# Transposing the turned keys once and copying them to both row halves out of PSUM

## The reference, cut to what matters

```python
def global_axial_attention(q, k, v, q_gain, k_gain, ang2d):
    ...
    q = apply_rope(rms_norm(q, q_gain, QK_EPS), ang2d) * (HEAD_DIM ** -0.5)
    k = apply_rope(rms_norm(k, k_gain, QK_EPS), ang2d)
    ...
        s = jnp.einsum('bqkgd,bskd->bkgqs', qblk, k)
        p = jax.nn.softmax(s, axis=-1)
        return jnp.einsum('bkgqs,bskd->bqkgd', p, v)

def window_sink_attention(q, k, v, sink, ang1d):
    ...
    k = apply_rope(k, ang1d)
    ...
        s = jnp.einsum('bqkgd,bskd->bkgqs', qblk, kblk)
        s = jnp.where(mask, s, -jnp.inf)
```

## Time and profile before

| | |
|---|---|
| three runs | 1204.88, 1205.07, 1205.17 us; median 1205.07 us |
| the profiled execution | 1204.98 us, span 1203.0 us, so 1.98 us around the span |
| busy share of the span | PE 99%, PEld 81%, POOL 49%, DVE 44%, ACT 40% |
| mean granted TensorE clock | 0.998 of full speed |

### The profile page before, as it was taken

How to read it: one execution, slowest core, us unless ns; L and a number is a source line. 1 busy time by engine, 2 the same in 40 slices (tenths; PEclk the granted TensorE clock), 3 DMA queues, 4 the chain that set the end, 5 groups by cost and what they waited for, 6 DMA issues and landing times.

```text
span 1203.0 us, 16482 instructions
## 1 busy us (share of the span) xinstructions
PE 1186.2 (99%) x5784; PEld 971.0 (81%) x5784; DVE 524.5 (44%) x1094; ACT 483.5 (40%) x890; POOL 585.3 (49%) x338
## 2 busy tenths in 40 slices
PE   7999999999999999999999999999999999999997
PEld 6787778888888888888888777788888888888886
DVE  7777857522121234211587788374221122431107
ACT  3457763244343333323144777433443343332310
POOL 6565754455444444343254756634554443434330
PEclk9999999999999999999999999999999999999999
DMA  6321213344333332223132202333433333322301
GB/s 223 87 71 54 89 53 106 122 125 138 97 95 87 105 106 88 88 92 104 54 80 79 73 34 71 140 105 88 140 106 103 99 93 96 97 74 102 105 35 70
DMA packets 121753, 113.45 MB, mean 94 GB/s; under 512 B 6752, under 2 KB 97888, under 8 KB 121696
## 3 DMA queue, kind: packets, MB, share of 16 engines
q1 hardware_dynamic: 121696, 112.71, 30.1%
HBM read 110.60 MB, written 2.10 MB: 94 GB/s over the span
## 4 chain that ended last, share of the span: by engine, by line
PE 95%; DVE 1%; POOL 1%; DVEq 1%; DMA 1%; issue 0%; SPq 0%
PE ps L1238 29%; PE ps L1240 28%; PE ps L1239 28%; PE ps L1404 3%; PE ps L1390 3%; PE ps L1378 1%; PE ps L1380 1%; PE ps L1248 1%; PE ps L1361 1%; POOL w_lo L544 1%; DMA x<-in_x_prompt_dram 1%; POOL ln_r L540 0%; DVEq L886 0%; DVEq L932 0%; PE ps L1415 0%
## 5 line engine op out<-in xcount | busy, mean ns | idle before, releaser
L534 POOL TENSOR_TENSOR w_lo<-raw,w_hi 128x1024 fp32r<-128x1024 f32 x188 | 453.1, 2412 | 404.6 <-ACT w_hi L645 404.5
L1238 PE MATMUL ps<-xt_hi,w_hi 128*128 128x512 f32 x704 | 273.9, 389 | 0.0
L1239 PE MATMUL ps<-xt_lo,w_hi 128*128 128x512 f32 x704 | 273.9, 389 | 0.0
L1240 PE MATMUL ps<-xt_hi,w_lo 128*128 128x512 f32 x704 | 273.9, 389 | 0.0
L645 ACT ACTIVATE w_hi<-raw 128x1024 fp32r<-128x1024 f32 x188 | 197.8, 1055 | 132.2 <-PE ps L1240 61.4
L1238 PE MATMUL ps<-w_hi,stat 128*128 128x512 f32 x480 | 187.8, 391 | 0.0
L1239 PE MATMUL ps<-w_lo,stat 128*128 128x512 f32 x480 | 187.1, 390 | 0.0
L1240 PE MATMUL ps<-w_hi,stat 128*128 128x512 f32 x480 | 187.1, 390 | 0.0
L1238 PEld LDWEIGHTS ps<-xt_hi,w_hi 128*128 128x128 f32 x704 | 132.2, 188 | 27.5
L1239 PEld LDWEIGHTS ps<-xt_lo,w_hi 128*128 128x128 f32 x704 | 132.2, 188 | 27.4
L1240 PEld LDWEIGHTS ps<-xt_hi,w_lo 128*128 128x128 f32 x704 | 132.2, 188 | 27.3
(11 more groups left out here) (123 smaller groups left out, 1323.7 us busy)
## 6 DMA issues: line engine op xcount, KB each, us to landing
raw<-in_w_up_dram SPq DMA_DIRECT2D x88, 512.0 KB, 3.8
raw<-in_w_down_dram SPq DMA_DIRECT2D x44, 512.0 KB, 3.2
raw<-in_w_in_dram SPq DMA_DIRECT2D x22, 512.0 KB, 3.7
raw<-in_w_out_dram SPq DMA_DIRECT2D x16, 512.0 KB, 3.3
raw<-in_w_ple_gate_dram SPq DMA_DIRECT2D x16, 512.0 KB, 3.3
scratch<-in_ln_g_dram SPq DMA_DIRECT2D x5, 512.0 KB, 4.1
scratch<-in_ln_b_dram SPq DMA_DIRECT2D x5, 512.0 KB, 6.0
raw<-in_w_ple_dram SPq DMA_DIRECT2D x4, 512.0 KB, 3.3
```

The costliest lines, as they stand in the source:

```text
L534: pool.tensor_tensor(w_lo[:, n, :], raw[:, n % RAW, :], w_hi[:, n, :].bitcast(F32), ALU.subtract).then_inc(w_split.sem, 1)
L1238: pe.matmul(out, a[0], b[0], start=first, stop=False)
L1239: pe.matmul(out, a[0], b[1], start=False, stop=False)
L1240: return pe.matmul(out, a[1], b[0], start=False, stop=last)
```

## The change

The kept keys are written once by `rotate`: 128 columns where 256 stood. In `rot` of stripes 1 and 2 TensorE then transposes three blocks, with the two key heads in one of them, head `v` in rows 64 v to 64 v + 63. `qkt_evac` copies each head to both row halves by itself: four copies of 64 rows by 128 columns (head v = 0, 1, to half odd = 0, 1), and `qkt_lo` makes the four low parts likewise. Nothing else is changed: the queries' copies, the semaphores and the order of the steps stay.

```diff
-        def k_parts(c, u):
+        def k_part(c, u, v):

             at = 0 if c == 1 else 256
-            first = 4 * (c - 1)
-            return (ps[:, TRB + u % 2, at:at + 256].rearrange("p (v n) -> p v n", v=KV), slice(first, first + 2),
-                    slice(first + 2, first + 4))
+            return ps[HD * v:HD * v + HD, TRB + u % 2, at:at + P]
+
+        def k_home(c, v, lo, odd, t):
+
+            return k_split[HD * odd:HD * odd + HD, k_block(c - 1, v, lo), t * P:(t + 1) * P]
...
                     if c:
-                        src, hi_at, _ = k_parts(c, u)
-                        act.activation(k_split[:, hi_at, cols_t], src, ACT.Copy)
+                        for v in range(KV):
+                            for odd in range(2):
+                                act.activation(k_home(c, v, 0, odd, t), k_part(c, u, v), ACT.Copy)
...
-                        dve.tensor_tensor(out[:, 0:256].rearrange("p (v e d) -> p v e d", v=KV, e=2),
...
+                        dve.tensor_tensor(out[:, 0:128].rearrange("p (v d) -> p v d", v=KV),
...
-                        dve.tensor_tensor(out[:, 0:256], bank[:, 0:256], turned[:, 0:256], ALU.add)
...
-                        dve.tensor_tensor(out[:, 256:512].rearrange("p (v e d) -> p v e d", v=KV, e=2),
...
+                        dve.tensor_tensor(out[:, 0:384], bank[:, 0:384], turned[:, 0:384], ALU.add).then_inc(rot_done.sem, 1)
...
                     if c:
-                        src, hi_at, lo_at = k_parts(c, u)
-                        dve.tensor_tensor(k_split[:, lo_at, cols_t], src, k_split[:, hi_at, cols_t].bitcast(F32), ALU.subtract)
+                        for v in range(KV):
+                            for odd in range(2):
+                                dve.tensor_tensor(k_home(c, v, 1, odd, t), k_part(c, u, v),
+                                                  k_home(c, v, 0, v, t).bitcast(F32), ALU.subtract)
...
-                        for k in range(4):
+                        for k in ((0, 1, 2, 3), (0, 2, 3), (0, 1, 2))[c]:
                             ins = pe.transpose(ps[:, TRB + u % 2, k * P:(k + 1) * P], rot[:, t % 2, k * P:(k + 1) * P], ident[:, :])
```

More of the change, by code:

```diff
@@ L983, in rotate @@
                         dve.wait_ge(qk_rstd.sem, qk_rstd.at(layer, n + 1))
-                        shape = [P, KV, 2, HD]
-                        dve.tensor_tensor(out[:, 0:256].rearrange("p (v e d) -> p v e d", v=KV, e=2),
-                                          bank[:, 0:128].rearrange("p (v d) -> p v d", v=KV).unsqueeze(2).to_broadcast(shape),
-                                          rqk[:, 1, t, 0:KV].unsqueeze(2).unsqueeze(3).to_broadcast(shape),
+                        dve.tensor_tensor(out[:, 0:128].rearrange("p (v d) -> p v d", v=KV),
+                                          bank[:, 0:128].rearrange("p (v d) -> p v d", v=KV),
+                                          rqk[:, 1, t, 0:KV].unsqueeze(2).to_broadcast([P, KV, HD]),
                                           ALU.mult).then_inc(rot_done.sem, 1)
@@ L994, in rotate @@
                         dve.drain()
-                        dve.tensor_tensor(out[:, 0:256], bank[:, 0:256], turned[:, 0:256], ALU.add)
-                        shape = [P, KV, 2, HD]
-                        dve.tensor_tensor(out[:, 256:512].rearrange("p (v e d) -> p v e d", v=KV, e=2),
-                                          bank[:, 256:384].rearrange("p (v d) -> p v d", v=KV).unsqueeze(2).to_broadcast(shape),
-                                          turned[:, 256:384].rearrange("p (v d) -> p v d", v=KV).unsqueeze(2).to_broadcast(shape),
-                                          ALU.add).then_inc(rot_done.sem, 1)
+                        dve.tensor_tensor(out[:, 0:384], bank[:, 0:384], turned[:, 0:384], ALU.add).then_inc(rot_done.sem, 1)
                 def qkt_lo(c, t):
```

## The result

The changed kernel takes 1212.61 us (median of 6 runs, 1212.17 to 1213.76), the kernel before 1205.12 us (6 runs, 1204.66 to 1205.71). The ratio is 1.0063, with a 95% interval of 1.0052 to 1.0074: 7.5 us slower where 6.8 were forecast.

The account below looks back on a forecast made before the run. TensorE, busy 99% of the span, was taken as the bound. Per layer -0.22 + 2.13 - 0.22 + 1.72 = +3.41 us, two layers +6.8, gave 1211.9 us; the range went from 1207.3 to 1216.

Parts of the forecast that it names:

- The price of a piece: Key pieces of 64 rows by 128 columns: 0.30 us on VectorE, 0.28 on ScalarE, with no overlap.
- Rounds 1 to 5: Early attention rounds: exps(3) ends 2.30 us later, so scores(5) starts late, +2.13 us per layer.
- Rounds 7 to 15: At rot(2, 0) and rot(2, 1): the longer copies stay hidden, TensorE gains 0.22 us per layer.
- Rounds 15 to 23: After rot(2, 2): exps(21) ends 2.22 us later, against 0.50 of room before scores(23), +1.72 us per layer.
- Stripe 1, t = 0 and 1: First two steps of stripe 1: the longer copies stay hidden, TensorE gains 0.22 us per layer.
- Sum: Whole kernel: +3.41 us per layer, +6.8 for two layers, 1211.9 us.
- the last term: The +1.72 us per layer forecast for rounds 15 to 23.
- What would show it: Profile signs: three-transpose steps, pieces at 0.28 and 0.30, runs of 1.1 and 1.2 us, TensorE waits released by ScalarE's exponentials.
- Overlap on ScalarE alone: Rival: ScalarE's pieces overlap, VectorE's don't, +0.38 in place of +0.86 us per step; 1209.9 us, chance 0.13.
- on both: Rival: pieces overlap on both ScalarE and VectorE; 1207.3 us, chance 0.08.
- the price of 256 columns: Rival: a key piece costs what 64 rows by 256 columns do, 0.43 and 0.38 us; 1218.1 us, chance 0.06.
- the other side: Rival: a piece's fixed part is hidden, only columns count, 0.12 and 0.10 us; faster, 1203.6 us, chance 0.04.

Follow-up runs that it names:

- e9: Kernel before, both engines' key parts cut into four pieces of 64 rows by 128 columns, ordered low, low, high, high: 1211.23 us, ratio 1.0054.
- e2: Kernel before with only ScalarE's key copy cut into four pieces of 64 rows by 128 columns: 1207.68 us, ratio 1.0023.
- e3: Kernel before with only VectorE's key subtraction cut into four pieces of 64 rows by 128 columns: 1210.81 us, ratio 1.0051.
- e5: Changed kernel with VectorE's long key parts put behind maxima(1) and maxima(3), and rotate(2, 0) one round later: 1207.05 us, ratio 1.0019.
- e6: Kernel before with the change made only in the steps t = 0 and 1 of both stripes: 1204.52 us, ratio 1.0000.
- e8: Changed kernel with sumsq(1) moved on TensorE behind scores(23): 1212.47 us, ratio 1.0064.
- e1: Changed kernel, but key parts made by one wide copy and one wide subtraction from one block (scores read wrong keys): 1203.04 us, ratio 0.9986.

## Why the prediction was right, point by point

- **The price of a piece: right.** 0.287 and 0.272 us in the groups of the changed kernel (64 of each), against 0.30 and 0.28; runs of four in 1.20 and 1.11 us, against 1.20 and 1.12. That rows don't set the price and columns do holds. That the change of the row half stops the overlap, taken from two pairs in the earlier trace rows, is shown by e9 against e2 and e3.
- **Rounds 1 to 5: right**, +2.17 and +2.19 against +2.13. `exps(3)` ended 0.17 us ahead of `scores(5)` before; it now ends at 85.94 and `scores(5)` starts at 85.99. e5 shows that the path runs through VectorE's maxima. The prediction was wrong about POOL's `normalise(1)`, which it called due with more room: the transposes of group 1's probabilities waited 0.25 us for it at 85.07. That cost nothing further, because `scores(5)` behind them still had to wait for `exps(3)`.
- **Rounds 7 to 15: right in the changed kernel**, -0.32 for three transposes. e6 has less, -0.05, so the cover there is thinner than the forecast said; that the changed kernel meets no wait there because TensorE is late already is argued, not shown.
- **Rounds 15 to 23: right mechanism, the size too small**, +2.22 against +1.83. `exps(21)` was forecast right: it ends at 142.10, 22.41 us behind `scores(16)`, against 136.88 - 116.79 = 20.09 before. That is 2.32 later, and the forecast was 2.22 + 0.11 = 2.33 (`scores(16)` comes 0.11 earlier by the transpose saved in rot(2, 2)). Wrong was "where `scores(23)` started at 137.38": the 0.50 us between the end of `exps(21)` and that start were taken for room, but TensorE was at work in them, most of the time with `sumsq(1)`, which stands in its list between. In the kernel before:

  ```profile
  137.02 0.50 PE L1415 MATMUL ps<-ones,hbuf 128*128 128x1 f32 x4
  ```

  In the changed kernel `sumsq(1)` waits for VectorE's copy of the probabilities, late by the same cause; the copy, then the end of `exps(21)`:

  ```profile
  141.22 0.69 DVE L1040 COPY late<-ps 128x512 f32<-128x512 f32 x1
  ```

  ```profile
  141.90 0.20 ACT L718 ACTIVATION_READ_ACCUMULATOR scratch<-ps,neg_max 128x1 f32 x1
  ```

  The copy ends at 141.91, `sumsq(1)` starts at 142.06 and `scores(23)` 0.44 later, at 142.50. That is again 0.40 us behind the end of `exps(21)`, so only 0.10 of the 0.50 us were room, and 0.39 us a layer, 0.8 in all, came on top. e8 shows it: without `sumsq(1)` between, the stretch is +1.89, close to the forecast, and its work comes on top behind `scores(23)`. In e2 and e3 the room is missing too.
- **Stripe 1, t = 0 and 1: about right**, -0.15 ahead of layer 1 against -0.22.
- **Sum.** With the last term mended, 2 x (-0.15 + 2.18 - 0.32 + 2.21) = 7.8 us against 7.5 between the medians; the start to `scores(0)`, which lies between 69.5 and 70.4 us in the other kernels' profiles, is not known better than that.
- **What would show it.** The transposes, the groups and the runs of four are as named. Of TensorE's waits, "released by ScalarE's exponentials" held for four of the seven of a layer, ahead of `scores(3)` to `scores(5)` and `scores(19)`. The other three stand where none was named: for the copy at L1040, ahead of `sumsq(1)` and not of `scores(23)`; for VectorE's query parts (L1011), 0.44 us ahead of transposes of probabilities at 138.36; and for GpSimd's `normalise` (L566).
- **The rivals.** Overlap on ScalarE alone, on both, and the price of 256 columns fall with the runs of four; the other side falls with e1, which has the gain only because the pieces are gone. Nothing is taken back later either: from `scores(23)` to `scores(31)` of layer 0 it is 24.33 us against 24.32, and only 0.15 us go ahead of layer 1.

## What to carry to other kernels

Before an instruction is cut into pieces, look at the start rows of each piece's operands against those of the one ahead: where the half stayed, the next piece started 0.07 to 0.14 us before the one ahead had ended; where the destination's half changed, alone or with the source's, each piece cost its whole duration. Work saved on the engine that sets the time is worth nothing in a stretch where it will wait for the engine that was given the work; read the room there from the timelines, and count as room only time in which the waiting engine is idle, not the time in which it does other work ahead of the wait. If long work must stay, put it behind what is waited for: the new order alone turned 7.5 us of loss into 2.5.

## What was not expected of the hardware

A ScalarE copy of 64 columns takes 245 ns, hardly less than the 272 of 128 columns, yet four in a row fill only 0.56 us: short copies over all rows are cheap by overlap, not by duration. And TensorE's granted clock stood at 0.50 for some microseconds of the start in seven of the twelve profiles, longest in that of the changed kernel, and not in that of the kernel before. TensorE had done nothing from 20 to 21 us in all twelve, so what decides it stays open.
